# Low parts of the experts' down weights made by one engine, and three norms computed tile by tile inside the projections ahead of them

## What is computed

```
def rms_norm_2(x, g):
    xf = x.astype(jnp.float32)
    y = xf * lax.rsqrt(jnp.mean(xf * xf, axis=-1, keepdims=True) + EPS)
    return (y * g.astype(jnp.float32)).astype(x.dtype)

# first block: mixer, then PEER experts
        x = x + gt1 * mixed
        h2 = rms_norm(x, g_norm2[l]) * (1.0 + sc2) + sh2
# second block: mixer, cross attention, mixture of 32 experts
        x = x + hybrid_mixer(rms_norm_2(x, norm_mix_g[l]), ...)
        x = x + cross_attention(rms_norm_2(x, norm_x_g[l]), ...)
        x = x + hierarchical_moe(rms_norm_2(x, norm_ffn_g[l]), ...)
# one expert
        return (jax.nn.silu(x_blk @ w1[e]) * (x_blk @ w3[e])) @ w2[e]
```

## Time and profile before

| | us |
|---|---|
| median of 3 runs | 3195.26 (3185.93 to 3196.11) |
| the profiled execution | 3198.86, of which span 3197.0 |
| PE busy | 2746.9 (86% of the span) |
| DVE busy | 2089.7 (65%) |
| ACT busy | 1328.5 (42%) |
| POOL busy | 933.0 (29%) |
| experts' stage, first to last matmul | 2557 to 3155 |

### The profile page before, as it was taken

How to read it: one execution, slowest core, us unless ns; L and a number is a source line. 1 busy time by engine, 2 the same in 40 slices (tenths; PEclk the granted TensorE clock), 3 DMA queues, 4 the chain that set the end, 5 groups by cost and what they waited for, 6 DMA issues and landing times. The chain is left out here.

```text
span 3197.0 us, 35282 instructions
## 1 busy us (share of the span) xinstructions
PE 2746.9 (86%) x12794; PEld 2220.9 (69%) x12794; DVE 2089.7 (65%) x3462; ACT 1328.5 (42%) x2009; POOL 933.0 (29%) x623
## 2 busy tenths in 40 slices
PE   4976879798968999999999977986688399999993
PEld 3444668557747999999999965753566378888882
DVE  4334537799957777767777765326423289999994
ACT  2112532115633333333333333244233188788872
POOL 1000023140023333334443313411111135465542
PEclk8977989899989999999999988987899599999997
DMA  7610012233579888888888843210120389999983
GB/s 245 236 56 17 1 55 80 89 136 151 211 274 313 304 280 289 291 290 299 295 286 292 303 135 106 79 56 4 52 80 1 146 337 360 364 365 362 361 348 135
DMA packets 219913, 646.27 MB, mean 202 GB/s; under 512 B 43132, under 2 KB 100220, under 8 KB 206204
## 3 DMA queue, kind: packets, MB, share of 16 engines
q1 hardware_dynamic: 173324, 501.86, 43.2%
q0 software_dynamic: 46448, 142.67, 13.4%
HBM read 614.47 MB, written 55.12 MB: 209 GB/s over the span
## 5 line engine op out<-in xcount | busy, mean ns | idle before, releaser
L2690 ACT ACTIVATE ex_w_hi<-expert_raw 128x1024 fp32r<-128x1024 f32 x384 | 374.9, 1052 | 105.8 <-DMA expert_raw<-in_w 104.6
L209 POOL TENSOR_TENSOR w_lo<-ring,w_hi 128x512 fp32r<-128x512 f32 (+1 forms) x136 | 173.1, 1304 | 568.7 <-ACT w_hi L199 568.7
L1574 PE MATMUL bank<-v_hi,peer_w_hi 128*128 128x512 f32 x768 | 300.6, 391 | 21.2 <-DVE peer_w_lo L1680 21.2
L2736 DVE TENSOR_TENSOR ex_w_lo<-expert_raw,ex_w_hi 128x1024 fp32r<-128x1024 f32 x256 | 305.2, 1253 | 0.4 <-ACT ex_w_hi L2690 0.3
L1574 PE MATMUL bank<-v_lo,peer_w_hi 128*128 128x512 f32 x768 | 301.0, 392 | 0.0
L1574 PE MATMUL bank<-v_hi,peer_w_lo 128*128 128x512 f32 x768 | 301.0, 392 | 0.0
L2607 POOL TENSOR_TENSOR ex_w_lo<-expert_raw,ex_w_hi 128x1024 fp32r<-128x1024 f32 x64 | 214.4, 3369 | 265.1 <-ACT ex_w_hi L2690 265.1
L1562 PE MATMUL bank<-h_hi,u_hi 128*128 128x384 f32 x832 | 279.2, 336 | 3.0 <-DVE u_lo L1641 3.0
L1562 PE MATMUL bank<-h_hi,u_lo 128*128 128x384 f32 x832 | 279.0, 335 | 0.0
L1562 PE MATMUL bank<-h_lo,u_hi 128*128 128x384 f32 x832 | 278.8, 335 | 0.0
L1549 POOL DMA_INDIRECT got_rows<-in_u_rows,diff x128 | 183.2, 1431 | 318.4 <-DVE got_rows L1648 290.2
(11 more groups left out here) (481 smaller groups left out, 6244.2 us busy)
## 6 DMA issues: line engine op xcount, KB each, us to landing
expert_raw<-in_w SPq DMA_DIRECT2D x96, 2048.0 KB, 9.0
v_in<-in_expert_v SPq DMA_DIRECT2D x128, 512.0 KB, 7.0
u_in<-in_u_tiles SPq DMA_DIRECT2D x104, 512.0 KB, 5.2
ada_in<-in_w_ada SPq DMA_DIRECT2D x48, 512.0 KB, 5.1
gates_by_key<-spread SPq DMA_DIRECT2D x6, 4096.0 KB, 11.7
gate_in<-gates_by_key SPq DMA_DIRECT2D x384, 64.0 KB
ring<-in_w_in SPq DMA_DIRECT2D x11, 2048.0 KB, 8.5
early_u<-in_u_tiles SPq DMA_DIRECT2D x24, 512.0 KB, 3.8
```

The source lines that it names most:

```text
L209: eng.tensor_tensor(g.w_lo[:, k, 0:cols], g.ring[u % RING][:, k, 0:cols], g.w_hi[:, k, 0:cols].bitcast(F32), ALU.subtract).then_inc(s["z_f ...
L1574: last = pe.matmul(g.bank[2 + o][:, :], x[:, par, e, i * P:(i + 1) * P], v[:, par, e, c], start=(first and n == 0), stop=(final and n == 3 ...
L2690: act.activation(hi[kind][:, c, :], whole(u, c), ACT.Copy).then_inc(s["r_hi"], 1)
L2736: dve.tensor_tensor(lo[which][:, c, :], whole(u, c), hi[which][:, c, :].bitcast(F32), ALU.subtract).then_inc(s["r_lo"], 1)
```

## The change

Two things are changed. First, in the experts' stage DVE makes all four chunks of the low part of w2 at the place where it made two, and POOL only gathers and scatters. Second, the three norms behind `mix_out` are no longer stages: each token tile is squared, scaled, transposed and written to `ht` within `mix_out`, as soon as its group has been added. For place C the rows times the gain are made and stored there too, tile by tile. The norm ahead of the hybrid mixer stays a stage.

```diff
+class NextNorm:
+    def act_stats(self, act, i):
+        act.wait_ge(self.summed, self.first_sum + i + 1)
+        act.activation(self.xn[:, i, :], g.x[:, i, :], ACT.Square, accum_out=self.ss[:, i:i + 1]).then_inc(s["f_sq"], 1)
+        act.wait_ge(s["f_sq"], i + 1)
+        act.activation(self.rms[:, i:i + 1], self.ss[:, i:i + 1], ACT.Sqrt, scale=1.0 / D, bias=g.eps[:, :]).then_inc(s["f_root"], 1)
+    def dve_scale(self, dve, i):
+        dve.wait_ge(s["f_root"], i + 1)
+        dve.reciprocal(self.rs[:, i:i + 1], self.rms[:, i:i + 1]).then_inc(s["f_rs"], 1)
+        dve.wait_ge(s["f_rs"], i + 1)
+        dve.tensor_scalar(self.xn[:, i, :], self.g.x[:, i, :], self.rs[:, i:i + 1], None, ALU.mult).then_inc(s["f_xn"], 1)
+    def pe(self, pe, i):
+        pe.wait_ge(s["f_xn"], i + 1)
...
+        for k in range(DC):
+            last = pe.transpose(self.bank(i, k // 4)[:, k % 4 * P:(k % 4 + 1) * P], self.xn[:, i, k * P:(k + 1) * P], self.g.ident[:, :])
+            if k % 4 == 3:
+                last.then_inc(s["f_flipped"], 1)
+    def act_out(self, act, i):
...
+        for k in range(4 if self.shift is None else DC):
+            if k % 4 == 0:
+                act.wait_ge(s["f_flipped"], 2 * i + k // 4 + 1)
+            dst, src = self.g.ht[:, k, i * P:(i + 1) * P], self.bank(i, k // 4)[:, k % 4 * P:(k % 4 + 1) * P]
...
+    def dve_out(self, dve, i):
...
+        dve.wait_ge(s["f_flipped"], 2 * i + 2)
+        for k in range(4, DC):
...
+            dve.tensor_scalar(dst, src, self.scale[:, k:k + 1], None, ALU.mult).then_inc(s["f_dve"], 1)
-def mix_out(g, chunks, first_unit, gate, local):
+def mix_out(g, chunks, first_unit, gate, local, xn, scale=None, shift=None, gain_src=None, store=None):
         def _(sp):
+            norm.sp(sp)
+            if store is not None:
+                sp.dma_start(row_gain[:, :], gain_src.unsqueeze(0).partition_broadcast(P)).then_inc(s["e_gain"], 16)
             g.prefetch(sp, first_unit + 2 + RING)
+            if store is not None:
+                for i in range(TT):
+                    sp.wait_ge(s["e_gained"], i + 1)
+                    for c in range(2):
+                        row = c * T + i * P
+                        sp.dma_start(store[row:row + P, :], xn[:, i, :]).then_inc(g.rows_stored, 16)
                 products.pe(pe, n, g.bank[n % 4][:, :])
+                if n > TT:
+                    norm.pe(pe, n - TT - 1)
+            norm.pe(pe, TT - 1)
             products.act_unit(act, 1)
+            for i in range(TT + 1):
+                if i < TT:
+                    norm.act_stats(act, i)
+                if i:
+                    norm.act_out(act, i - 1)
+        def finish_rows(dve, i):
+            if shift is None:
+                norm.dve_out(dve, i)
+            if store is not None:
...
+                dve.tensor_tensor(xn[:, i, :], xn[:, i, :], row_gain[:, :], ALU.mult).then_inc(s["e_gained"], 1)
+                    if u:
+                        norm.dve_scale(dve, i)
+                        if i:
+                            finish_rows(dve, i - 1)
                     n += 1
+            finish_rows(dve, TT - 1)
# route, on SP
-                sp.dma_start(gain[:, :], a["norm_ffn_g_2"][0:1, :].partition_broadcast(P)).then_inc(s["q_gain"], 16)
...
-                sp.wait_ge(s["q_gained"], TT)
-                for c in range(2):
-                    sp.dma_start(x_rows[c * T:(c + 1) * T, :].rearrange("(i p) d -> p i d", p=P), xn_tiles[:, :, :]).then_inc(s["q_x"], 16)
+                sp.wait_ge(g.rows_stored, 2 * TT * 16)
                 begin(sp)
# run_experts, on SP and PE the waits follow; on POOL and DVE:
-                def down_low(n):
-                    u = EXPERT_LOADS.index((n, 2))
-                    for c in range(CH // 2):
...
-                    down_low(n)
                     if n:
                         scatter(n - 1)
                 def down_low(n):
                     u = EXPERT_LOADS.index((n, 2))
-                    for c in range(CH // 2, CH):
+                    for c in range(CH):
```

More of the change, by code:

```diff
@@ L920, in mix_out @@
+def mix_out(g, chunks, first_unit, gate, local, xn, scale=None, shift=None, gain_src=None, store=None):
     nc = g.nc
     tmp = local.enter_context(nc.sbuf_tensor(fresh("mix_tmp"), [P, 2, BANK], F32))
-    with stage(nc, "e_flipped e_added e_dve" + Products.SEMS) as (block, s):
+    row_gain = local.enter_context(nc.sbuf_tensor(fresh("row_gain"), [P, D], F32)) if store is not None else None
+    with stage(nc, "e_flipped e_added e_dve e_gain e_gained" + Products.SEMS + NextNorm.SEMS) as (block, s):
@@ L2235, in cross_attention @@
         with ExitStack() as local:
-            mix_out(g, lambda k: y[:, :, k * P:(k + 1) * P], first_unit + 2, None, local)
+            rows = qt[:, :, :].rearrange("p k t -> p (k t)").rearrange("p (i d) -> p i d", d=D)
+            mix_out(g, lambda k: y[:, :, k * P:(k + 1) * P], first_unit + 2, None, local, rows, gain_src=a["norm_ffn_g_2"][0], store=x_rows)
 RG = NG + NE
@@ L2242, with route @@
 RAW = 3
-def route(g, begin, xn_tiles, x_rows, table, slot, weight, slots, over):
+def route(g, begin, table, slot, weight, slots, over):
     nc, a = g.nc, g.a
@@ L2274, in route @@
         rows = sb("list_rows", [P, P])
-        gain = sb("gain_row", [P, D])
         count, most = sb("count", [P, NE]), sb("most", [P, 1])
         whole8 = [P, TT, 8]
-        with stage(nc, "q_w q_pool q_ready q_zero q_mm q_dve q_pair q_red q_exp q_exp2 q_hits q_pos q_slot q_sent q_clear q_rows q_flip q_x q_gain q_gained") as (block, s):
+        with stage(nc, "q_w q_pool q_ready q_zero q_mm q_dve q_pair q_red q_exp q_exp2 q_hits q_pos q_slot q_sent q_clear q_rows q_flip") as (block, s):
             @block.sync
@@ L2341, in _ @@
                 step = InOrder(dve, s["q_dve"])
-                dve.wait_ge(s["q_gain"], 16)
-                for i in range(TT):
-                    dve.tensor_tensor(xn_tiles[:, i, :], xn_tiles[:, i, :], gain[:, :], ALU.mult).then_inc(s["q_gained"], 1)
                 dve.wait_ge(s["q_mm"], 1)
@@ L2565, in run_experts @@
         names = " ".join(f"r_{n}{p}" for n in ("x", "st") for p in range(2))
-        with stage(nc, names + " r_zero r_xt r_xhi r_xlo r_hi r_lo r_h1 r_h3 r_act r_z r_zt r_zhi r_zlo r_lo2 r_lo2v r_y r_yc") as (block, s):
+        with stage(nc, names + " r_zero r_xt r_xhi r_xlo r_hi r_lo r_h1 r_h3 r_act r_z r_zt r_zhi r_zlo r_lo2 r_y r_yc") as (block, s):
             used = ("r_h1", "r_h3", "r_y")
@@ L2917, in mixture @@
         over = sb("over_flag", [P, 1], I32)
-        gain = sb("moe_gain", [P, DC])
         raw = [sb(fresh("expert_raw"), [P, DC, BANK]) for _ in range(RAW)]
@@ L2924, in begin @@
                 load_expert(sp, a, raw, raw_in, u)
-        with ExitStack() as local:
-            xn = local.enter_context(nc.sbuf_tensor("moe_xn", [P, TT, D], F32))
-            with ExitStack() as inner:
-                norm_transposed(g, None, None, inner, gain_src=a["norm_ffn_g_2"][0], keep=xn, gain_keep=gain)
-            route(g, begin, xn, x_rows, table, slot, weight, slots, over)
+        route(g, begin, table, slot, weight, slots, over)
         with ExitStack() as local:
@@ L2979, in second_mixer @@
         with ExitStack() as local:
-            mix_out(g, mixed, first_unit + 8, None, local)
+            xn = local.enter_context(nc.sbuf_tensor("cross_xn", [P, TT, D], F32))
+            mix_out(g, mixed, first_unit + 8, None, local, xn, gain_src=a["norm_x_g_2"][0])
 def build(nc, a):
@@ L3019, in build @@
         with ExitStack() as local:
-            mix_out(g, mixed, 5, gate_row[:, 0, :], local)
-        with ExitStack() as local:
-            norm_transposed(g, col[:, 24:32], col[:, 16:24], local, keep=proj[:, :, 0:D])
+            mix_out(g, mixed, 5, gate_row[:, 0, :], local, proj[:, :, 0:D], col[:, 24:32], col[:, 16:24])
         proj_ctx.close()
@@ L3040, in build @@
         second_mixer(g, 15)
[L3041 to L3042 removed]
+        x_rows = nc.dram_tensor("moe_x", (2 * T, D), F32).ap()
+        cross_attention(g, 25, mem_kt, mem_v, x_rows)
+        mixture(g, a["out"], x_rows)
 def layout(inputs):
```

60 lines of the change are left out of this document (43 added, 17 removed).

## The result

| | us |
|---|---|
| kernel before, median of 4 (lowest to highest) | 3190.6 (3182.62 to 3196.11) |
| changed kernel, median of 4 (lowest to highest) | 3147.7 (3143.19 to 3150.45) |
| ratio, 95% interval | 0.9866, 0.9838 to 0.9894 |
| profiled execution of the changed kernel, its span | 3147.41, 3145.2 |
| forecast (range) | 3163.6 (3153 to 3178) |

What follows compares the result with a forecast made beforehand. The prediction took DVE's own chain to set the experts' round, with three non-overlapped gaps behind `mix_out`. Experts -12.1, A -6.6, B -7.7, C -5.3 sum to -31.7: from 3195.3 to 3163.6 us, range 3153 to 3178.

Steps and rivals of the forecast that it cites:

- place C: Third gap behind `mix_out`, ahead of `route`: 16.49 us falls to 8.2, transposes +2.0, router's loads +1; -5.3 us (-8 to -2).
- The experts' term: Experts' stage: holds of down go and the last expert gains; -12.1 us, 0 to -14.3.
- 0.51 us later in place of 0.227, so 0.28 us is lost: Passage from up w3 to down in a round: PE's first matmul of down is held, losing 0.28 us.
- Of the 12.2 us I take 10: Experts' 31 passages, excess 12.2 us: 10 would go, as 1.9 us of lead covers only part of the long holds.
- the last expert: End of the experts' stage, PE idle 8.56 us: low part of z ready earlier, 2.1 us gained.
- I count nothing: PE's granted clock in the three gaps behind `mix_out`: each place still has a gap, so 0 (0 to -2 in all).
- Place A: First gap behind `mix_out`: 17.29 us falls to 8.7, transposes add 2.0; -6.6 us (-9 to -1).
- the 2.0 of the working: Inside `mix_out`, PE's eight transposes behind each of groups 5 and 6 add 2.0 us at each place.
- Place B: Second gap behind `mix_out`: 15.33 us falls to 5.6, transposes add 2.0; -7.7 us (-9 to -5).
- The loads: Rival, experts' stage: loads stay at 358 GB/s, so the steady 10 us do not come; 3173.6 us, chance 0.12.
- POOL's gathers: Rival, experts' rounds: POOL's gathers and scatters hold DVE; 3194 us, the case as a whole about 3200, chance 0.04.
- More than counted: Rival: shorter gaps keep PE's clock up and all 12.2 us of the experts' holds go; 3157 us, chance 0.07.

Runs made afterwards that it cites:

- pool_beside: The changed kernel plus four 128x512 subtractions a round on POOL, on a small tile no other engine touches; 3173.82 us (0.9956).
- experts_only: The kernel before with one edit: VectorE makes all four low chunks of w2, the norms stay where they were; 3172.38 us (ratio 0.9954).
- dve_plus2: The changed kernel plus four unneeded 128x512 subtractions a round on VectorE ahead of the low part of z; 3176.58 us (0.9975).
- again: The changed kernel once more with no edit, beside the kernel before; 3142.56 against 3184.91 us (0.9865).

## Why the prediction was wrong

**What bounds.** Right. VectorE's closed chain set the round, POOL's halves made it slow (pool_beside shows the cause by itself), and PE was late next.

**The experts' term, -12.1, was mis-sized: -20.0 by the traces** (-14.7 by the times of experts_only, see above). It makes 7.9 of the 11.2 us by which the gain of 42.9 is above the 31.7 forecast. Three steps of it failed. "0.51 us later in place of 0.227, so 0.28 us is lost" looked at one interval; the second matmul comes late too, in 27 of the 31 passages, and what it and the third lose, 3.1 us, is most of the 4.8 behind the passages; another 0.9 was lost at the fourth and fifth. The prediction had the right number in its own text, a round of 18.16; it took the floor as 18.16 - 0.28 where 72 matmuls and 12 transposes without a hold take 17.74. "Of the 12.2 us I take 10": all 12.1 went, since z is now 4.3 us early, not 1.9. ACT also begins w2 11.6 us ahead of the down that wants it (2948.99 for 2960.6), where it was 9.7, which I had held fixed. And the last expert gave 2.4 + 0.7 where 2.1 was said; "I count nothing" for the clock was said of the three gaps, and this idle was not looked at for it.

**Place A, -6.6, was -7.95.** The gap of 8.7 was 7.4: a piece with gain and shift took 5.69 / 16 = 0.36 us, halfway between the plain 0.28 and the 0.43 taken. The transposes cost the 2.0 of the working. No tile was late: the eight transposes of tile 0 stand at 433.41, right behind a matmul at 433.19. ACT's table load took 1.28 us again (430.75), the root began at 432.05, 0.02 behind it; so here too no drain shows.

**Place B, -7.7, was -7.65. Place C, -5.3, was -6.4.** Gap 8.1 for 8.2, wait for the router's loads +1.15 for +1, `mix_out` +2.15 for 2.0. What was missed is in `route`, where I put the gain at 0: the experts' first loads start 4.3 us behind the stage's start in place of 14.4, and are done before POOL scatters the pairs; from the last scatter to the read of the lists pass 8.3 us in place of 9.7. That the loads' traffic is the reason is argued, not shown.

**Rivals.** The loads don't bound: 376 GB/s. POOL's gathers don't hold VectorE: chunks stay at 1.22 us, and at 1.21 in dve_plus2, where it is POOL that waits. "More than counted", 0.07, with 3157, was nearest: all 12.2 did go, but its other cause, the clock kept up in the shorter gaps, did not come (in 455 to 462, 2302 to 2310 and 2456 to 2465 us it is granted at 0.50), and its price was too small as well.

**The base.** 3195.3 was a median of three; with a fourth execution it is 3190.6, and 17 others gave 3186.4. By the steps as found, 3190.6 - 41.9 = 3148.7. The range had no term for the base. Its lower end, 3153, is what the bounds of the text give together: -14.3, -9, -9, -8, and -2 for the clock, so 3195.3 - 42.3. Places A, B and C stayed inside theirs; the experts, at -20.0, did not, and nearly the whole reserve of the others went into that. From a base of 3190.6 that end is 3148.3, still above the 3147.7 measured, so the base alone doesn't explain the miss, though 4.7 of its 5.3 us are that.

## What to carry to other kernels

Don't split subtractions of SBUF data between VectorE and POOL when VectorE has room in the round: of 5.2 us of POOL's work VectorE lost 2.6 (pool_beside) to 3.7 (the kernel before), and the cure was worth 15 to 20 us in one stage and 3 us in each of three first units of dense products. Price a hold by the round it makes against the round without it, not by the interval at its first matmul, and add the clock where PE stands idle for microseconds. And put the base's own scatter into the range.

## What the runs showed of the hardware

POOL and VectorE in the changed kernel's first `mix_out`, one short overlap after another:

```profile
395.01 1.27 POOL L210 TENSOR_TENSOR w_lo<-ring,w_hi 128x512 fp32r<-128x512 f32 x1 [1.35 <-ACT w_hi L200]
397.02 1.28 POOL L210 TENSOR_TENSOR w_lo<-ring,w_hi 128x512 fp32r<-128x512 f32 x1 [0.74 <-ACT w_hi L200]
...
416.59 10.47 POOL L210 TENSOR_TENSOR w_lo<-ring,w_hi 128x512 fp32r<-128x512 f32 x8 [16.25 <-ACT w_hi L200]
...
395.05 1.77 DVE L210 TENSOR_TENSOR w_lo<-ring,w_hi 128x512 fp32r<-128x512 f32 x1
396.75 1.28 DVE L216 TENSOR_TENSOR ht_lo<-bank,ht_hi 128x512 fp32r<-128x512 f32 x2
397.95 0.90 DVE L210 TENSOR_TENSOR w_lo<-ring,w_hi 128x512 fp32r<-128x512 f32 x1
```

- VectorE stands while POOL subtracts. Its subtraction at 395.05 ends 0.54 us behind POOL's (396.28), that at 397.95 ends 0.55 behind POOL's (398.30); alone it takes 0.68. The Trainium skill (SBUF — State Buffer, SBUF: two separate sides) has the other engine blocked for a whole instruction, and these rows agree but for some 0.14 us of VectorE's 0.68 that lay beside POOL's. In pool_beside 4.63 and 5.2 us of work took 8.1 together, not 9.8: some 0.2 us of each of the eight instructions still lay beside the other's.
- Of VectorE's subtractions only those with both operands in SBUF were held. The two from PSUM at 396.75 take their usual 1.28 us with POOL at work from 397.02. In the kernel before three low parts of z (2819.11, 2890.99, 3127.94) lay wholly beside a subtraction of POOL and took 0.68 or 0.69 us. So the low part of z was never slow itself, only the chunks ahead of it.
- POOL's issue of a gather grows from 1.06 us to 2.93 in dve_plus2, where VectorE hardly rests, at no cost to VectorE (chunks at 1.21 us).
- Unchanged stretches differ from trace to trace: one in the first block took about 156.3 or 160.2 us (once 158.6), another 957.2 to 962.8. Two executions can be 10 us apart with nothing changed (run `again`: 3140.36 to 3154.12).
